# Routing an encoder layer's tokens: router scores taken from x, and the first gathers ahead of the rest of the table

## The chip, the cores and the metric

The kernel runs on one NeuronCore of a Trainium2 chip. The time is the device time of one execution in microseconds (us), and lower is better. The five engines of the core appear here as PE (TensorE, matrix products), DVE (VectorE), ACT (ScalarE), POOL (GpSimd) and SP (SyncE, which here only issues transfers). PEld is PE's loading of stationary operands, and a "q" behind an engine's name (SPq, PEldq) is its instruction sequencer. PE's clock is granted at one of two levels, 2.4 GHz (shown as 1.00) or 1.2 GHz (0.50).

## What is computed

An encoder layer on 768 tokens (256 of a prompt, 512 of a sample) of width 1024, all in fp32. The part that the change touches is the second half, a mixture of experts in two levels:

```
x = x + m @ w_out[l]
h = rms_norm(x, norm2_g[l])
g_logits = h @ w_group + b_group          # 4 groups
e_all    = h @ w_expert + b_expert        # 4 x 8 experts
g_sel = argmax(g_logits); top_v, top_j = top_k(e_logits of the group, 2)
gates = p_g * softmax(top_v)
hid = silu(x_b @ w_gate[e]) * (x_b @ w_up[e])   # per block of gathered rows
y   = hid @ w_down[e]
```

`rms_norm(x, g)` is x times 1/sqrt(mean(x²) + eps), one factor per token, times g, one factor per column.

## The kernel before

Tokens lie in NT = 6 tiles of 128 rows. An attention and a convolution stage fill the first 285 us. Then comes the output product: 24 groups of 12 matmuls each (`out`, line 1143), each adding 512 columns of one tile to `x` through a DVE instruction (`px`, line 1721). When a tile is complete, ACT squares and sums it (`sq2`, L1473), POOL makes the norm's factor `r2` of it in two instructions (`root2`, L851 and L852), DVE writes the normed tile `h2` (L1728), PE transposes it in eight products (`turn_h2`, L1156), ACT copies the transposed tile out of PSUM (`turned_h2`, L1480), and PE multiplies it by the router's weights `wr`, 36 columns (`logits`, L649). SP stores each tile of `h2` twice to `h_rows` in HBM (L770), because rows are gathered from there later. The order of all these steps on each engine comes from `plan()`, a list scheduler with estimated costs: a step is placed when its predecessors are finished by those costs. `tnh`, `tch` and `lgt` are its names for turn, copy and logits.

Where PE has to wait it multiplies constants (`stay_busy(n)`, n products of 128x128, L1163). One such stretch of 16 lies between the last output product and the logits of tile 4.

After the logits (semaphore `lg_done`) DVE and PE take turns for some 25 us: adding the bias (L1802), choosing groups and experts, counting them, ordering the experts by load, and placing each token in a block of 64 rows. The blocks' row lists come out of a one-hot product on PE (L1225, two halves), which raises `idx_ps`. DVE then writes a `table` of integers (L1861 to L1871) with the experts' order, their first blocks and ends, and two loop counts; then it turns the row lists into indices (`idx_of` for the first two blocks, L1876; `idx` for all, L1878); then it computes the gates (to L1888), which PE spreads over the blocks in a second one-hot product (L1233). The table's readers load integers from it into registers (`value_load`): POOL its loop counts (L899, L900), PE the blocks of each expert (L1295, L1296), SP an expert's number and end (L743, L744).

POOL then gathers the first two blocks of rows (L910, an indirect transfer). DVE waits for the gates and the first gather and copies the block (L1935), PE turns it (`turn_rows`, L1240), DVE copies that out (L1897), and PE starts the first expert: gate and up products in two halves of k (L1249, L1252), then the down products (L1286, L1287).

Weights, 6 MB for each of 32 experts, are streamed by SP (L736) into three slots. The first three experts' are loaded ahead: part during the output product, the other 9.5 MB behind the last store of `h2`. Every later load waits for PE to have finished with the slot; the first of them waits for `gu_half`, which PE raises when the first half of the first expert's gate and up products is done.

Of the kernel before, what the change touches and what calls it, by code (L numbers as in the profile page):

```python
# [34 lines left out]
P = 128  # L35
D = 1024
# [123 lines left out]
def parts():  # L160
# [222 lines left out]
def encoder(nc, x_prompt, x_sample, norm1, w_in, rpb, vectors, w_out, norm2, router_w, router_b,  # L383
# [15 lines left out]
    with ExitStack() as ctx:  # L399
# [57 lines left out]
        h2T = mid[:, NT * D:NT * D + 2 * D].rearrange("p (b k n) -> p b k n", b=2, k=KD)  # L457
# [32 lines left out]
        br = sb("br", [P, NR])  # L490
        ident = sb("ident", [P, P])
# [25 lines left out]
        def after(n):  # L517
# [79 lines left out]
        sq2, root2, h2_ready, h2t_done, h2t_ready, lg_done = (  # L597
            sem("sq2"), sem("root2"), sem("h2_ready"), sem("h2t_done"), sem("h2t_ready"), sem("lg_done"))
# [46 lines left out]
        def logits(pe, t):  # L645

            pe.wait_ge(h2t_ready, t + 1)
            for k in range(KD):
                mm = pe.matmul(ps[:, 6, t * NR:(t + 1) * NR], h2T[:, t % 2, k, :], wr[:, k, :],  # L649
                               start=(k == 0), stop=(k == KD - 1))  # L650
            mm.then_inc(lg_done, 1)
# [3 lines left out]
        def _(sp):  # L655
# [18 lines left out]
            sp.dma_start(wr[:], router_w.rearrange("p (k n) -> p k n", k=KD)).then_inc(small_in, 16)  # L674
            sp.dma_start(br[:], bass.AP(router_b.tensor, 0, [[0, P], [1, NR]])).then_inc(small_in, 16)
# [104 lines left out]
            sp.wait_ge(h2t_done, NT)  # L780
# [22 lines left out]
        def _(pool):  # L803
# [181 lines left out]
        def _(pe):  # L985
# [162 lines left out]
            def turn_h2(t):  # L1148
                pe.wait_ge(h2_ready, t + 1)
                if t == 1:  # L1150
                    pe.wait_ge(ssc_ready, 1)
                if t >= 2:
                    pe.wait_ge(h2t_ready, t - 1)
# [4 lines left out]
                mm.then_inc(h2t_done, 1)  # L1158
# [6 lines left out]
            for what, *a in ORDER:  # L1165
# [22 lines left out]
                elif what == "po":  # L1188
                    out(*a)
                    if a[0] == len(OUT) - 1:  # L1190
                        pe.wait_ge(x2_done, max(g for g in range(len(OUT)) if OUT_BANK[g] == 7) + 1)
                        stay_busy(16)
                elif what == "tnh":
                    turn_h2(*a)
# [24 lines left out]
            stay_busy(12)  # L1219
# [8 lines left out]
            stay_busy(8)  # L1228
# [7 lines left out]
            stay_busy(4)  # L1236
# [56 lines left out]
            turn_rows()  # L1293
            def expert(place, s, target):
# [33 lines left out]
        def _(act):  # L1328
# [146 lines left out]
            def turned_h2(t):  # L1475
                act.wait_ge(h2t_done, t + 1)
                if t >= 2:
                    act.wait_ge(lg_done, t - 1)
                bank = 4 * (1 - t % 2)
                nc.scalar.activation(h2T[:, t % 2, :, :].rearrange("p k n -> p (k n)"),  # L1480
                                     ps[:, bank:bank + 2, :].rearrange("p a b -> p (a b)"),
                                     ACT.Copy).then_inc(h2t_ready, 1)

            for what, *a in ORDER:
# [26 lines left out]
                elif what == "sq2":  # L1511
                    squares_of_x2(*a)
                elif what == "tch":
                    turned_h2(*a)
# [54 lines left out]
        def _(dve):  # L1569
# [207 lines left out]
            dve.wait_ge(small_in, 32)  # L1777
# [24 lines left out]
            link(V.tensor_tensor(lg[:], ps[:, 6, 0:NT * NR].rearrange("p (t n) -> p t n", t=NT), same(br[:], NR), ALU.add))  # L1802
# [62 lines left out]

            link(V.tensor_scalar(even[:], even[:], ends[0:1, E:], None, ALU.is_lt))
# [5 lines left out]

            dve.wait_ge(idx_ps, 1)
            link(V.tensor_scalar(nobody[:], ps[0:BLK, 5, 0:NB], 0.0, float(4 * T), ALU.is_equal, ALU.mult))
            for q in range(2):
                V.scalar_tensor_tensor(idx_of[q][:], nobody[:, q:q + 1], -1.0, ps[0:BLK, 5, q:q + 1], ALU.add, ALU.add  # L1876
                                       ).then_inc(idx_ready, 1)
            V.scalar_tensor_tensor(idx[:], nobody[:], -1.0, ps[0:BLK, 5, 0:NB], ALU.add, ALU.add).then_inc(idx_ready, 1)  # L1878
# [144 lines left out]
```

## Time and profile before

| | us |
|---|---|
| median of 3 runs | 938.34 (937.21 to 940.13) |
| profiled execution | 941.61 |
| its span, first to last instruction | 939.8 |
| PE busy in the span | 856.7 |
| DVE busy | 427.1 |
| ACT busy | 249.2 |
| POOL busy | 146.5 |

The profile is of one execution, and times in its views are counted from the start of the span. The other 1.8 us of that execution lie around the span. A share of busy time is a mean over stages with different limits, so it has to be read stage by stage.

### The profile page before, as it was taken

The page shows a single profiled execution, that of the slowest core. Times are in us where ns is not written, and L with a number is a line of the kernel's source. Part 1 is how long each engine was busy: PE and PEld are TensorE (multiplying, and loading weights), DVE is VectorE, ACT ScalarE, POOL GpSimd, SP SyncE. Part 2 cuts the span into 40 slices and gives each one's busy share as a digit, 9 for nine tenths or more (in the row PEclk, how much of TensorE's full clock was granted, in tenths as well). Part 3 has the DMA queues.
Part 4 walks back from the last instruction along what each step waited for, and adds up shares of the span by engine and source line. Part 5 has one row for each costly group of instructions (what it writes and reads, how often), then busy time and mean ns, then how long its engine had stood idle before and what let it go on. Part 6 is the DMA issues. An engine that isn't in the chain of part 4 may idle for free.

```text
span 939.8 us, 16091 instructions
## 1 busy us (share of the span) xinstructions
PE 856.7 (91%) x5980; PEld 588.0 (63%) x5981; DVE 427.1 (45%) x639; ACT 249.2 (27%) x486; POOL 146.5 (16%) x287
## 2 busy tenths in 40 slices
PE   3989999999869999699999789999999999899984
PEld 2879978777648889655554445565555555455541
DVE  5398988866997443622222112222222212222256
ACT  5313164565565122011111011111111111111121
POOL 4200010000000110122221212222122222121203
PEclk9989999999979999989999999999999999999998
DMA  7443445221085355969999999999999999999984
GB/s 204 121 113 102 150 153 190 91 80 45 1 224 224 153 217 193 368 238 404 402 390 395 414 402 399 406 390 397 400 403 410 404 401 379 394 387 407 395 331 137
DMA packets 80892, 265.80 MB, mean 283 GB/s; under 512 B 18089, under 2 KB 43945, under 8 KB 56280
## 3 DMA queue, kind: packets, MB, share of 16 engines
q1 hardware_dynamic: 63232, 245.10, 68.7%
q0 software_dynamic: 7808, 18.56, 5.7%
q10 hardware_dynamic: 9816, 1.66, 1.0%
q8 instruction: 23, 0.38, 0.2%
q14 instruction: 13, 0.11, 0.0%
HBM read 247.52 MB, written 27.08 MB: 292 GB/s over the span
## 4 chain that ended last, share of the span: by engine, by line
PE 51%; DMA 21%; SPq 16%; DVE 7%; issue 3%; ACT 1%; ACTq 0%; POOLq 0%; POOL 0%; DVEq 0%
SPq L736 15%; DMA big<-in_w_up 13%; PE ps L1021 13%; PE ps L1249 7%; PE ps L1143 7%; DMA ring<-in_w_up 6%; PE ps L1286 5%; PE ps L1017 4%; PE ps L1252 3%; DVE big L1637 2%; PE ps L1240 1%; PE ps L1040 1%; PE ps L1070 1%; PE ps L1049 1%; PE ps L649 1%
## 5 line engine op out<-in xcount | busy, mean ns | idle before, releaser
L1252 PE MATMUL ps<-ring,big 128*64 128x256 f32 x704 | 158.4, 383 | 7.1 <-DMA ring<-in_w_up 7.1
L1249 PE MATMUL ps<-ring,big 128*64 128x256 f32 x704 | 158.8, 383 | 1.8 <-DVE big L1897 1.2
L1021 PE MATMUL ps<-hT,w_split 128*128 128x512 f32 (+1 forms) x768 | 145.2, 344 | 4.1 <-DVE hT L1593 3.6
L1908 DVE TENSOR_TENSOR big<-ps,big 64x256 f32<-64x256 f32 x78 | 33.2, 426 | 242.4 <-ACT big L1534 242.4
L1252 PE MATMUL ps<-big 128*64 128x256 f32 x544 | 122.0, 380 | 16.5 <-DMA big<-in_w_up 16.5
L1021 PEld LDWEIGHTS ps<-hT,w_split 128*128 128x128 f32 x768 | 118.0, 190 | 25.6 <-issue 11.3
L1249 PEld LDWEIGHTS ps<-ring,big 128*64 128x64 f32 x704 | 96.8, 138 | 57.7 <-issue 14.1
L1249 PE MATMUL ps<-big 128*64 128x256 f32 x544 | 123.1, 380 | 0.5 <-DMA big<-in_w_gate 0.5
L1637 DVE SCALAR_TENSOR_TENSOR big<-big,vec 128x783 f32<-128x783 f32 x116 | 119.6, 1031 | 3.0
L1252 PEld LDWEIGHTS ps<-ring,big 128*64 128x64 f32 x704 | 96.9, 138 | 14.4 <-DMA ring<-in_w_up 9.4
L1534 ACT ACTIVATE big<-ps 64x256 f32<-64x256 f32 x78 | 29.3, 376 | 268.7 <-PE ps L1252 268.7
L1252 PEld LDWEIGHTS ps<-big 128*64 128x64 f32 x544 | 73.4, 137 | 36.8 <-DMA big<-in_w_up 22.6
L1249 PEld LDWEIGHTS ps<-big 128*64 128x64 f32 x544 | 73.2, 137 | 31.4 <-issue 8.1
L1917 DVE TENSOR_SCALAR big<-ps,gate_of 64x512 f32<-64x512 f32 x39 | 29.5, 756 | 124.4 <-PE ps L1287 124.3
L1286 PE MATMUL ps<-ring,big 128*64 128x512 f32 x176 | 80.4, 599 | 0.1
L1287 PE MATMUL ps<-ring,big 128*64 128x512 f32 x176 | 80.5, 599 | 0.0
L1143 PE MATMUL ps<-wo_split,hT 128*128 128x512 f32 x288 | 70.2, 402 | 2.1 <-issue 2.1
L922 POOL COPY to_of<-idx 64x1 uint32 x37 | 18.8, 508 | 309.8 <-DVE big L1917 309.8
L1143 PEld LDWEIGHTS ps<-wo_split,hT 128*128 128x128 f32 x288 | 54.9, 194 | 13.5 <-issue 2.1
L1286 PE MATMUL ps<-big 128*64 128x512 f32 x136 | 62.3, 599 | 0.1
L1287 PE MATMUL ps<-big 128*64 128x512 f32 x136 | 62.4, 599 | 0.0
L1546 ACT ACTIVATE big<-ps,gate_of 64x512 f32<-64x512 f32 x39 | 26.6, 682 | 131.8 <-PE ps L1287 131.8
(236 smaller groups left out, 1132.5 us busy)
## 6 DMA issues: line engine op xcount, KB each, us to landing
ring<-in_w_gate SPq DMA_DIRECT2D x44, 1024.0 KB, 29.0
ring<-in_w_up SPq DMA_DIRECT2D x44, 1024.0 KB, 29.8
ring<-in_w_down SPq DMA_DIRECT2D x44, 1024.0 KB, 30.1
big<-in_w_gate SPq DMA_DIRECT2D x20, 1024.0 KB, 29.8
big<-in_w_up SPq DMA_DIRECT2D x20, 1024.0 KB, 30.7
big<-in_w_down SPq DMA_DIRECT2D x20, 1024.0 KB, 29.8
w_raw<-in_w_in SPq DMA_DIRECT2D x20, 512.0 KB, 3.9
results<-spare POOLq DMA_DIRECT2D x12, 512.0 KB, 2.9
```

The lines of the kernel that those rows point to most:

```text
L736: sp.dma_start(to[:, ks, :], src).then_inc(landed, 16)
L1017: mm = pe.matmul(ps[:, n % 2, 0:2 * P], hT[:, k // 4, hi_h, k % 4, g * P:(g + 1) * P], split_of(2 * c)[:, :, hi_w, k, :], **flags)
L1021: mm = pe.matmul(ps[:, n % 2, 0:size], w_split[:, sub, hi_w, k, :], hT[:, k // 4, hi_h, k % 4, cols], **flags)
L1143: mm = pe.matmul(ps[:, OUT_BANK[g], :], mT[:, part, hi_m, k, t * P:(t + 1) * P], wo_split[n % 2][:, hi_w, k, :], start=(k == 0 and m == 0) ...
L1249: pe.matmul(ps[0:BLK, 6 * h, 0:FH], xT[:, k, :], gate_w[s][:, k, fs], start=(k == 0), stop=(k == KD - 1))
L1252: mm = pe.matmul(ps[BLK:2 * BLK, 6 * h + 1, 0:FH], xT[:, k, :], up_w[s][:, k, fs], start=(k == 0), stop=(k == KD - 1))
L1286: pe.matmul(ps[0:BLK, 2, :], hbT[:, k, :], down_w[s][:, k, 0:512], start=(k == 0), stop=(k == KF - 1))
L1287: mm = pe.matmul(ps[BLK:2 * BLK, 3, :], hbT[:, k, :], down_w[s][:, k, 512:1024], start=(k == 0), stop=(k == KF - 1))
L1534: nc.scalar.activation(sG[:, h * FH:(h + 1) * FH], ps[0:BLK, 6 * h, 0:FH], ACT.Silu).then_inc(sg_ready[h], 1)
L1637: link(nc.vector.scalar_tensor_tensor(conv[:, j % 2, :], z, w, conv[:, j % 2, :], ALU.mult, ALU.add))
L1908: nc.vector.tensor_tensor(hb[:, fs], ps[BLK:2 * BLK, 6 * h + 1, 0:FH], sG[:, fs], ALU.mult).then_inc(hb_ready[h], 1)
L1917: nc.vector.tensor_scalar(yb2[q][:, 512:1024], ps[BLK:2 * BLK, 3, :], gate_of[q][BLK:2 * BLK], None, ALU.mult).then_inc(evacuated, 1)
```

## The change

The router's scores no longer wait for the norm. PE transposes `x` itself, the norm's column factors are multiplied into `wr` once, and the row factor `r2` is put onto the scores in one more DVE instruction. On DVE the indices come before the last six instructions of the table, and POOL asks for the first two gathers before it loads its loop counts. The counts of `stay_busy` change at five places and one is added. `norm2` is loaded a second time, one factor per partition and chunk (128x8 single values).

```diff
-            in_line(("tnh", t), [("h2", t)] + ([("tch", t - 2)] if t >= 2 else []) + ([("sscc",)] if t == 1 else []))
+            in_line(("tnh", t), [("px", s)] + ([("tch", t - 2)] if t >= 2 else []) + ([("sscc",)] if t == 1 else []))
...
-            pe.wait_ge(h2t_ready, t + 1)
+            pe.wait_ge(x2t_ready, t + 1)
+            if t == 0:
+
+                pe.wait_ge(h2_ready, 1)
...
             sp.dma_start(wr[:], router_w.rearrange("p (k n) -> p k n", k=KD)).then_inc(small_in, 16)
+            sp.dma_start(n2_column[:], bass.AP(norm2.tensor, 0, [[1, P], [P, KD]]), allow_slow_non_contiguous=True).then_inc(small_in, 16)
...
-            pool.wait_ge(table_ready, 1)
-            pairs = pool.value_load(table[0:1, 3 * E:3 * E + 1], min_val=(E - 7) // 2, max_val=MAXPAIRS)
-            rest = pool.value_load(table[0:1, 3 * E + 1:3 * E + 2], min_val=2, max_val=3)
...
             for q in range(2):
                 pool.wait_ge(idx_ready, q + 1)
                 fetch(q)
+            pool.wait_ge(table_ready, 1)
+            pairs = pool.value_load(table[0:1, 3 * E:3 * E + 1], min_val=(E - 7) // 2, max_val=MAXPAIRS)
+            rest = pool.value_load(table[0:1, 3 * E + 1:3 * E + 2], min_val=2, max_val=3)
...
-            def turn_h2(t):
-                pe.wait_ge(h2_ready, t + 1)
+            def turn_x2(t):
+                pe.wait_ge(x2_done, OUT.index((OUT_CHUNKS - 1, t)) + 1)
...
-                                      h2[:, t, k * P:(k + 1) * P], ident[:])
+                                      x[:, t, k * P:(k + 1) * P], ident[:])
...
-                        stay_busy(16)
+                        stay_busy(2)
...
-            stay_busy(12)
+            stay_busy(13)
...
-            stay_busy(8)
+            stay_busy(14)
...
-            stay_busy(4)
+            stay_busy(8)
...
             turn_rows()
+            stay_busy(3)
             def expert(place, s, target):
...
                 if t == 0:
                     dve.wait_ge(norms_in, 16)
+                    dve.wait_ge(small_in, 48)
+                    link(nc.vector.tensor_tensor(wr[:], wr[:], n2_column[:].unsqueeze(2).to_broadcast([P, KD, NR]), ALU.mult))
...
-            link(V.tensor_tensor(lg[:], ps[:, 6, 0:NT * NR].rearrange("p (t n) -> p t n", t=NT), same(br[:], NR), ALU.add))
+
+            link(V.tensor_tensor(lg[:], ps[:, 6, 0:NT * NR].rearrange("p (t n) -> p t n", t=NT), over(r2[:], NR), ALU.mult))
+            link(V.tensor_tensor(lg[:], lg[:], same(br[:], NR), ALU.add))
...
+            dve.wait_ge(idx_ps, 1)
+            link(V.tensor_scalar(nobody[:], ps[0:BLK, 5, 0:NB], 0.0, float(4 * T), ALU.is_equal, ALU.mult))
+            for q in range(2):
+                V.scalar_tensor_tensor(idx_of[q][:], nobody[:, q:q + 1], -1.0, ps[0:BLK, 5, q:q + 1], ALU.add, ALU.add
+                                       ).then_inc(idx_ready, 1)
+            V.scalar_tensor_tensor(idx[:], nobody[:], -1.0, ps[0:BLK, 5, 0:NB], ALU.add, ALU.add).then_inc(idx_ready, 1)
+
             link(V.tensor_scalar(even[:], even[:], ends[0:1, E:], None, ALU.is_lt))
```

PE, from the second half of the output product to the end of the logits (128x512 are output products, 12 to a group; 128x128 from `ident` and `big` or `x` the turns; 128x36 the logits). Before:

```order
L1143 MATMUL ps<-wo_split,hT 128x512 x120
L1156 MATMUL ps<-ident,big 128x128 x8
L1143 MATMUL ps<-wo_split,hT 128x512 x12
L649 MATMUL ps<-wr,big 128x36 x8
L1156 MATMUL ps<-ident,big 128x128 x8
L1143 MATMUL ps<-wo_split,hT 128x512 x12
L649 MATMUL ps<-wr,big 128x36 x8
```

The same place on PE now:

```order
L1147 MATMUL ps<-wo_split,hT 128x512 x108
L1160 MATMUL ps<-ident,x 128x128 x16
L653 MATMUL ps<-wr,big 128x36 x8
L1147 MATMUL ps<-wo_split,hT 128x512 x12
L653 MATMUL ps<-wr,big 128x36 x8
L1147 MATMUL ps<-wo_split,hT 128x512 x24
L1160 MATMUL ps<-ident,x 128x128 x8
```

The turns of tiles 0 and 1 stand together, one group earlier, and the logits of tile 0 directly behind them; before, an output group lay between a turn and its logits. On ACT the copy of tile 0 still stands behind the squares of tile 1:

```order
L1472 ACTIVATE wo_split<-wo_raw 128x2048 x2
L1478 ACTIVATE big,ss<-x 128x1024 x2
L1485 ACTIVATE big<-ps 128x1024 x2
L1478 ACTIVATE big,ss<-x 128x1024
L1485 ACTIVATE big<-ps 128x1024
```

What moved on ACT is only the copy of tile 1, which now follows that of tile 0 at once.

DVE behind the first three instructions of the table, now (before, the rows from `even` to `table<-ends` stood first and those from `nobody` to `idx` last):

```order
L1872 TENSOR_SCALAR table<-ps 1x32
L1875 TENSOR_SCALAR nobody<-ps 64x58
L1877 SCALAR_TENSOR_TENSOR idx_of<-nobody,ps 64x1 x2
L1879 SCALAR_TENSOR_TENSOR idx<-nobody,ps 64x58
L1881 TENSOR_SCALAR even<-even,ends 1x24
L1882 TENSOR_REDUCE cnt<-even 1x1
L1883 SCALAR_TENSOR_TENSOR cnt<-cnt,ends 1x1
L1884 TENSOR_SCALAR cnt<-cnt 1x1
L1885 CAST table<-cnt 1x2
L1886 CAST table<-ends 1x32
```

The indices passed six small instructions, and the table is complete that much later. POOL behind the last root, now:

```order
L911 DMA big<-h_rows,idx_of 64x1024 x2
L936 TENSOR_LOAD table
L936 ISA x2
L937 TENSOR_LOAD table
L937 ISA x2
L917 COPY gate_of<-row_gates 128x1 x2
```

Before, the two loads with their checks stood ahead of the two gathers.

## Rows read from the trace of the kernel before

**Rows 1.** The page, second part: mean busy share of the DMA engines in 40 slices.

```profile
DMA  7443445221085355969999999999999999999984
```

**Rows 2.** Busy time by stretch: PE, PEld, DVE, ACT, POOL, granted clock, DMA share, GB/s.

```profile
800.00:900.00 100.00, 96.17 (x730) 55.98 (x728) 24.81 (x43) 15.54 (x39) 16.99 (x33) 1.00 1.00 397
```

**Rows 3.** SP's queue in order of time: start, us, transfers issued.

```profile
374.31 1.09 SPq L736 DMA_DIRECT2D big<-in_w_down  x2
408.73 0.36 SPq L736 DMA_DIRECT2D ring<-in_w_gate  x1
...
420.73 0.34 SPq L736 DMA_DIRECT2D ring<-in_w_gate  x1
```

**Rows 4.** The chain that ended last, around the logits: start, us, work.

```profile
332.41 0.88 PE ps L1156 x8
...
363.00 3.57 PE ps L1163 x32
...
369.22 1.03 ACT big L1480
370.30 1.99 PE ps L649 x16
372.31 0.40 DVE lg L1802
```

**Rows 5.** DVE and ACT in order of time, around tile 1's completion.

```profile
329.72 0.75 DVE L1721 SCALAR_TENSOR_TENSOR x<-ps,rc,x 128x512 f32<-128x512 f32 x1 [1.97 <-PE ps L1143]
...
331.48 0.18 ACT L1473 ACTIVATION_READ_ACCUMULATOR big<-x 128x1 f32 x1
```

**Rows 6.** PE and DVE in order of time, around the index.

```profile
390.55 0.91 PE L1225 MATMUL ps<-big,spare 128*64 128x58 f32 x24 [0.54 <-DVE big L1858]
...
390.82 0.18 DVE L1864 TENSOR_SCALAR table<-ps 1x32 int32<-1x32 f32 x1
...
392.14 0.20 DVE L1874 TENSOR_SCALAR nobody<-ps 64x58 f32<-64x58 f32 x1
392.38 0.21 DVE L1876 SCALAR_TENSOR_TENSOR idx_of<-nobody,ps 64x1 uint32<-64x1 f32 x2
```

**Rows 7.** The chain again, from the first gather to the first expert.

```profile
394.56 4.93 DMA big<-h_rows,idx_of
...
399.58 0.70 DVE spare L1935
...
402.76 0.68 PE ps L1249
```

**Rows 8.** Who waited for whom (us in total, times), and the gathers' landing times.

```profile
POOL big L910 <- POOL idx_of L903: 31.4, 37, 0.9
...
DMA to landing us min/median/max: 3.5/7.2/8.2
```

**Rows 9.** PE in order of time and its granted clock by 1 us (columns of Rows 2).

```profile
396.37 1.16 PE L1163 MATMUL ps<-lane,ident 128*128 128x128 f32 x8
400.41 1.11 PE L1240 MATMUL ps<-ident,spare 64*128 64x64 f32 x8 [2.88 <-DVE spare L1935]
...
416.91 0.38 PE L1249 MATMUL ps<-ring,big 128*64 128x256 f32 x1
...
400.00:401.00 1.00, 0.59 (x6) 0.62 (x6) 0.27 (x1) 0.00 (x0) 0.18 (x1) 0.62 0.00 0
...
407.00:408.00 1.00, 1.00 (x12) 0.63 (x10) 0.00 (x0) 0.00 (x0) 0.00 (x0) 0.96 0.00 0
```

**Rows 10.** PE's sequencer at the table: durations in ns (min/median/max), first and last start.

```profile
L1295 PEldq TENSOR_LOAD <-table x32: 298/303/502, 400.7 to 890.8; - x32
```

**Rows 11.** SP's queue at the start, and its loads of 1024 runs of 512 bytes.

```profile
33.76 0.48 SPq L676 DMA_DIRECT2D n<-in_norm  x1
39.59 28.35 SPq L661 DMA_DIRECT2D w_raw<-in_w_in  x5
...
L661 SPq DMA_DIRECT2D w_raw<-in_w_in x20: 367/373/596, 4.0 to 197.0; - x20
```

More of the change, by code:

```diff
@@ L456, in encoder @@
         h2 = mid[:, 0:NT * D].rearrange("p (t d) -> p t d", t=NT)
-        h2T = mid[:, NT * D:NT * D + 2 * D].rearrange("p (b k n) -> p b k n", b=2, k=KD)
+        x2T = mid[:, NT * D:NT * D + 2 * D].rearrange("p (b k n) -> p b k n", b=2, k=KD)
         slot2_gu, slot2_dn = big[:, (NT + 2) * D:(NT + 2) * D + 2 * KD * F], big[:, 0:KF * D]
@@ L490, in encoder @@
         br = sb("br", [P, NR])
+        n2_column = sb("n2_column", [P, KD])
         ident = sb("ident", [P, P])
@@ L596, in encoder @@
         wout_done, x2_done = sem("wout_done"), sem("x2_done")
-        sq2, root2, h2_ready, h2t_done, h2t_ready, lg_done = (
-            sem("sq2"), sem("root2"), sem("h2_ready"), sem("h2t_done"), sem("h2t_ready"), sem("lg_done"))
+        sq2, root2, h2_ready, x2t_done, x2t_ready, lg_done = (
+            sem("sq2"), sem("root2"), sem("h2_ready"), sem("x2t_done"), sem("x2t_ready"), sem("lg_done"))
         gd_ready, ge_ready, order_ready, order_ps, dd_ready, ex_ready, dest_ready, table_ready = (
@@ L645, in logits @@
         def logits(pe, t):
-            pe.wait_ge(h2t_ready, t + 1)
+            pe.wait_ge(x2t_ready, t + 1)
+            if t == 0:
+                pe.wait_ge(h2_ready, 1)
             for k in range(KD):
-                mm = pe.matmul(ps[:, 6, t * NR:(t + 1) * NR], h2T[:, t % 2, k, :], wr[:, k, :],
+                mm = pe.matmul(ps[:, 6, t * NR:(t + 1) * NR], x2T[:, t % 2, k, :], wr[:, k, :],
                                start=(k == 0), stop=(k == KD - 1))
@@ L779, in _ @@
             sp.wait_ge(h2_out, 32 * NT)
-            sp.wait_ge(h2t_done, NT)
+            sp.wait_ge(x2t_done, NT)
             load_some(2, 2, 4, 6)
@@ L1152, in turn_h2 @@
                 if t >= 2:
-                    pe.wait_ge(h2t_ready, t - 1)
+                    pe.wait_ge(x2t_ready, t - 1)
                 bank = 4 * (1 - t % 2)
@@ L1156, in turn_h2 @@
                     mm = pe.transpose(ps[:, bank + k // 4, (k % 4) * P:(k % 4 + 1) * P],
-                                      h2[:, t, k * P:(k + 1) * P], ident[:])
-                mm.then_inc(h2t_done, 1)
+                                      x[:, t, k * P:(k + 1) * P], ident[:])
+                mm.then_inc(x2t_done, 1)
             def stay_busy(products):
@@ L1191, in _ @@
                         pe.wait_ge(x2_done, max(g for g in range(len(OUT)) if OUT_BANK[g] == 7) + 1)
-                        stay_busy(16)
+                        stay_busy(2)
                 elif what == "tnh":
-                    turn_h2(*a)
+                    turn_x2(*a)
                     if a[0] == NT - 1:
@@ L1473, in squares_of_x2, with turned_x2 @@
                 nc.scalar.activation(junk, x[:, t, :], ACT.Square, accum_out=ss2[:, t:t + 1]).then_inc(sq2, 1)
-            def turned_h2(t):
-                act.wait_ge(h2t_done, t + 1)
+            def turned_x2(t):
+                act.wait_ge(x2t_done, t + 1)
                 if t >= 2:
@@ L1479, in turned_h2 @@
                 bank = 4 * (1 - t % 2)
-                nc.scalar.activation(h2T[:, t % 2, :, :].rearrange("p k n -> p (k n)"),
+                nc.scalar.activation(x2T[:, t % 2, :, :].rearrange("p k n -> p (k n)"),
                                      ps[:, bank:bank + 2, :].rearrange("p a b -> p (a b)"),
-                                     ACT.Copy).then_inc(h2t_ready, 1)
+                                     ACT.Copy).then_inc(x2t_ready, 1)
             for what, *a in ORDER:
@@ L1513, in _ @@
                 elif what == "tch":
-                    turned_h2(*a)
+                    turned_x2(*a)
             act.wait_ge(gd_ready, 1)
@@ L1776, in _ @@
             dve.wait_ge(lg_done, NT)
-            dve.wait_ge(small_in, 32)
             V = nc.vector
@@ L1871, in _ @@
             V.tensor_copy(table[0:1, 2 * E:3 * E], ends[0:1, 1:]).then_inc(table_ready, 1)
[L1873 to L1878, printed above, removed]
             dve.wait_ge(ge_ready, 1)
```

## The prediction, made before the result was known

> **What bounds the kernel now.** I read the page first, by slices [rows 1]: the DMA engines are only half busy before the experts (digits 3, 5, 5, 3 around 290 to 380 us), and from slice 18 to the end full. The table by stretch says the same [rows 2]: from 800 to 900 us their share is 1.00 at some 400 GB/s. PE is nearly full too (96 of 100 us), but it has what the weights give it. So from the first reload of weights on, the bytes that are left set the end, and what a change ahead of it is worth is read at one instant: SP's first reload, at 408.73 us [rows 3]. Whatever moves this instant moves the end by as much.
>
> Then I went back from it. The reload waits for half of the first expert's gate and up products, which start at 402.76 [rows 7]. They wait for the first gather, which is asked for at 394.56 and lands 4.93 us later. That one waits for the index, and this for the 18 us of turns between DVE and PE behind the logits, whose first instruction is at 372.31 [rows 4]. The change touches the logits, the index and the gather. I take them in this order.
>
> **Ahead of the last output group: a new stall.** The output product runs on PE without a gap. Group 15, tile 1's last, ends as its DVE instruction starts, 329.72 [rows 5]. Behind it PE now has the turns of tiles 0 and 1, 0.88 each [rows 4], done at 331.47, and then at once the logits of tile 0. These need ACT's copy of tile 0, and ACT has the squares of tile 1 first, which end at 331.48 + 0.18 = 331.66 [rows 5]. The copy takes 1.03, and PE followed such a copy 0.05 later [rows 4]: 332.74. PE stands for 1.27 us, and as nothing else was idle there, the last output group ends that much later. Before, an output group stood in between. The wait of tile 0's logits for `wr` and `h2` is covered: one multiplication of 128x288, between the 0.40 of the 128x216 one [rows 4] and perhaps 0.6, and one norm are done before 332.7. The later turns have a group between themselves and their copies: no stall. Cost: **+1.27**.
>
> **Behind it: 14 products less.** Between the last output group and the first table instruction PE is the late one: 16 products of constants take 3.57 us [rows 4], 0.223 each, then the logits of tile 4, the turn of tile 5, its copy, its logits. With 2 products instead of 16, 3.12 us go. What could be late next: the turn of tile 5 needs the last `px`, 0.8 us after the group; PE comes to it after 0.45 + 1.7. The copy of tile 5 needs ACT, busy with the squares until 2.0 after the group, while the turn ends at 3.0. The norm of tile 5, no longer in the way of PE, is done by DVE before the logits are. So the whole is won: **-3.12**. The scores get one more DVE instruction of the same size: 0.40 plus the 0.02 between two: **+0.42**. The chain behind it starts 1.43 us earlier, and its steps up to the index are unchanged: the fillers of 28, 6 and 13 products still end before what they wait for.
>
> **The index.** The second half of the index product runs from 390.55 to 391.46; DVE has finished the three table instructions at 391.00 and now takes the index at 391.50 instead of 392.14 [rows 6]. `idx_of` follows 0.24 later and is written at 391.9. POOL, now without table loads ahead, asks 0.85 us after its index is ready (31.4 us in 37 waits, [rows 8]): 392.75 instead of 394.56, **-1.81**. With the 1.43 the first gather is asked for at 391.32.
>
> **The landing.** Here the gain shrinks. The 4.93 us were measured at the end of the weights loaded ahead; the last of these are issued at 374.31 and after [rows 3]. They stand behind the norm of tile 5, so they move by the stall, 1.27 us later, while the gather moves 3.2 us forward, into their midst. Landings range from 3.5 to 8.2 us, with a median of 7.2, which stands for a full DMA [rows 8]. I take 7.2, since at 391 the engines are as full as in the expert phase: 398.52 instead of 399.49, **-0.97**. No row shows this first gather inside the burst, and 4.93 is the other value it can have; that is the first rival.
>
> The Trainium skill, page "DMA: Bandwidth & Descriptors", section "Queues, rings and completion order", says that a DMA engine goes round its queues packet by packet. By that rule a gather of few packets should pass the weights with little delay, which would give the first rival's time. The median of 7.2 in a full phase speaks against it.
>
> **From landing to the first product.** The block's copy starts at 399.58 and PE at 402.76 [rows 7], 3.18 later. Its sequencer loads the expert's numbers from 400.7 on [rows 10], while the turns of rows run (400.41, [rows 9]) and behind them, and I take these loads, two of 0.3 us with their checks, to be what is late rather than DVE's copy. The 3 new products stand ahead of them: at least their issue (12 instructions at the pace of the 16 that were issued in 0.3 us, 0.2), at most their run, 0.67. I take **+0.2**, as the sequencer is seen running ahead of the array. The Trainium skill, page "TensorE: Matmul & The Clock Gate", section "Architectural detail: the array is 16x 32x32, not 1x 128x128", gives PE's queue a depth of 64, which would hold all of them; with a queue that does not, it would be 0.67.
>
> **The clock.** The granted clock falls at 400.4, after 2.9 us without products, and is back at 407 [rows 9]. The first half of gate and up, 402.76 to SP's issue at 408.73, therefore takes 5.97; the next block, at full clock, takes 420.73 - 416.91 = 3.82 [rows 3, 9]. If the clock stays up, **-2.15**. The fillers grew for this: 14 products (3.1 us) behind the index, 8 (1.8 us) behind the gates. By my times the gate product ends at 395.4 (396.37 less 1.43, plus 0.46 for the instructions that now stand ahead of the gates), the filler at 397.2, and the turn of rows comes at 399.4: 2.2 us empty, and then 0.9 us more before the first expert. That is less than the 2.9 that preceded the fall, in the longest piece. I expect it to hold, with little room.
>
> **The rest.** The column load is 1024 runs of 4 bytes; loads of 1024 runs of 512 bytes are issued in 0.37 to 0.60 us, and SP has 5.3 us free there (34.24 to 39.59, [rows 11]). Between nothing and 5 us it is hidden, and it is first used 290 us later. Gates come 0.46 us later than the index gain alone would give, hidden by the landing. The table is ready later too; SP uses it only for the reload.
>
> **The sum.** Landing -0.97, three products +0.2, clock -2.15: the reload is issued at 405.8 instead of 408.7, **-2.9**. Against the profiled execution (941.61) that is 938.7. This execution was 3.3 above the median of the runs, so against the median, 938.34, it is **935.4**.
>
> **Rivals.**
> 1. *The gather passes the weights.* At 4.93 it lands at 396.3, and then PE's filler of 8 is late instead: the turn of rows cannot start before 397.2, 3.2 earlier than before. With +0.2 and the clock certainly held, -5.2: **933.1**. For it: this gather has no scatter in its own queue. Against: 7.2 in the full phase.
> 2. *The clock falls after all*, since 2.2 and 0.9 us are still empty. The gather's -0.97 and the +0.2 remain, -0.8, if the low stretch again lies half over the waits; if it falls only as the first expert starts, all 16 steps run low, 6.9 instead of 6.0, and it is +0.1 to +0.5. **938.2**, between 937.5 and 938.8.
> 3. *Slower: the weights ahead hold the gather back to the end.* The gather asked in mid-burst lands only when the burst, 1.27 us later than before, is through: 8.2 us (the longest row), 399.5. The same 2.9 us are then empty, the clock falls, later than before against the first expert, which runs 6.9 low, and the three products cost 0.67: 0 + 0.7 + 0.9 = +1.6, **939.9**. It decides against the change from a landing of 8 us on.
> 4. *The earlier reload does not reach the end.* If PE, at 96%, set the pace of the expert phase through its own work, it would still shift with its start; only a stall inside would eat the gain. **938.3**.
>
> **Chances.** Forecast 0.38, rival 1 0.24, rival 2 0.27, rival 3 0.07, rival 4 0.04. A measurement of this kernel can tell about 0.3%, 2.8 us, from no change. Rival 1 lies beyond it, the forecast just beyond (a little over half of it counts as faster), rivals 2 and 4 within, rival 3 within but for a spread of 1 to 2 us on top. Faster 0.47, same 0.46, slower 0.07. The range goes from rival 1 less 0.8 to rival 2's upper end plus 0.4: 932.3 to 939.2.
>
> **What the profile after would show.** PE idle for about 1.3 us at tile 0's logits, near 331.5, waiting for ACT. The first score instruction near 370.5, the index near 390.1, the first gather near 391.3 with a landing of 7 (rival 1: 5; rival 3: over 8). Granted clock 1.00 up to the first expert (rival 2: 0.50 there). SP's first reload near 405.8, and a DMA share of 1.0 from then on. The prediction is wrong if the stall is not there (1.3 better), if the routing chain between scores and index changed, or if the reload moves and the end does not.

## The result, and the profile after

The changed kernel takes **942.25 us** (median of 17 runs, 940.73 to 943.97) beside 938.99 for the kernel before (17 runs, 937.21 to 941.19). The ratio is 1.0033 (95% interval 1.0024 to 1.0042): slower by 3.3 us. 935.4 had been forecast, with a range up to 939.2. The profiled execution took 942.78 us with a span of 940.9, near the median. That of before, on which the sum was made, was 2.6 us above its median. One execution of a kernel shown further down (burst split, no stall) took 1233.76 us at a mean granted clock of 0.656; it is among the nine of that kernel's median (935.14), but not in its ratio.

First the instant that was to tell everything, SP's queue of the changed kernel in order of time (start, us, transfers issued); it answers to [rows 3]:

```profile
361.62 8.96 SPq L775 DMA_DIRECT2D h_rows<-big  x4
370.63 2.61 SPq L741 DMA_DIRECT2D ring<-in_w_up  x1
...
377.26 0.88 SPq L741 DMA_DIRECT2D big<-in_w_down  x2
410.46 0.36 SPq L741 DMA_DIRECT2D ring<-in_w_gate  x1
```

The first reload is issued at 410.46, where 405.8 was expected and before had 408.73. From there to the end of the span it is 530.4 us; before it was 531.1, and in all 14 traces of this document it lies between 529.5 and 531.1. So the step that whatever moves the reload moves the end by as much holds, and the loss lies ahead of it.

Next the chain that ended last (start, us, work), which answers to [rows 4, 7]:

```profile
330.62 0.76 DVE x L1726
...
331.40 1.15 ACT big L1478 x2
332.55 0.92 ACT big L1485
...
333.51 1.98 PE ps L653 x16
335.49 2.85 PE ps L1147 x12
...
365.56 0.44 PE ps L1167 x4
...
371.75 0.39 DVE lg L1809
...
384.87 4.64 PE ps L1167 x26
389.52 0.84 PE ps L1229 x24
...
391.42 0.22 DVE nobody L1875
...
392.78 8.39 DMA big<-h_rows,idx_of
...
401.26 0.70 DVE spare L1943
...
402.09 1.11 PE ps L1244 x8
403.20 1.58 PE ps L1167 x6
404.78 0.62 PE ps L1253
```

Three places differ from the forecast. The stall at tile 0's logits is there, as forecast (333.51). The gather is asked for 1.78 us earlier than before, but takes 8.39 us to land and arrives at 401.17, where before it arrived at 399.49. And the three new products (`L1167 x6`, each product has two records) take 1.58 us and end just before the first expert starts.

The windows of the changed kernel show what the gather waited for (columns of [rows 2]: PE, PEld, DVE, ACT, POOL, granted clock, DMA share, GB/s):

```profile
392.00:393.00 1.00, 1.00 (x11) 1.00 (x10) 0.83 (x6) 0.00 (x0) 0.22 (x1) 1.00 1.03 414
398.00:399.00 1.00, 1.00 (x10) 0.86 (x8) 0.00 (x0) 0.00 (x0) 0.00 (x0) 1.00 0.98 270
399.00:400.00 1.00, 0.05 (x1) 0.00 (x0) 0.00 (x0) 0.00 (x0) 0.00 (x0) 1.00 0.72 176
400.00:401.00 1.00, 0.00 (x0) 0.00 (x0) 0.00 (x0) 0.00 (x0) 0.00 (x0) 1.00 0.09 21
402.00:403.00 1.00, 0.91 (x8) 0.94 (x8) 0.00 (x0) 0.00 (x0) 0.18 (x1) 0.50 0.00 0
```

The DMA engines are full until 399, nearly empty from 400, and the gather's data is there 1 us after. The trace also has the packets by queue. q1 carries what SP issues, q0 the gathers (packets, MB, share of the 16 engines; first from 396 to 397, then from 397 to 398):

```profile
q1 hardware_dynamic: 56, 0.43, 100.8%
...
q1 hardware_dynamic: 40, 0.32, 86.9%
q0 software_dynamic: 20, 0.07, 19.6%
```

Until 397 the engines move no packet of the gather that was asked for at 392.78; from 397 on its packets go beside the last weights. Its first packet comes 4.3 us after the request, where in the kernel before it came 1.9 us after. So it did not pass the weights ahead of it; it came in at their end. PE has nothing to do meanwhile, and its clock is at the lower level when the rows are turned.

### The profile page after: what moved, and what is told of

The parts are those of the page before. It is cut to its first block, busy times and chain, and to the rows that moved or that the text cites. A ratio compares the mean times of both kernels' runs of the same rounds, so it can differ in the third digit from the quotient of the medians.

```text
span 940.9 us, 16096 instructions
## 1 busy us (share of the span) xinstructions
PE 860.8 (91%) x5980; PEld 591.6 (63%) x5981; DVE 428.4 (46%) x641; ACT 248.8 (26%) x486; POOL 146.1 (16%) x287
## 3 DMA queue, kind: packets, MB, share of 16 engines
q10 hardware_dynamic: 9816, 1.66, 0.9%
## 4 chain that ended last, share of the span: by engine, by line
PE 53%; DMA 24%; SPq 12%; DVE 6%; issue 2%; ACT 1%; ACTq 0%; POOL 0%; POOLq 0%; DVEq 0%
DMA big<-in_w_up 16%; PE ps L1025 13%; SPq L741 11%; PE ps L1253 8%; PE ps L1147 7%; PE ps L1290 5%; PE ps L1021 4%; DMA big<-in_w_down 3%; DMA ring<-in_w_up 3%; PE ps L1256 3%; DVE big L1642 2%; PE ps L1244 1%; PE ps L1044 1%; PE ps L1074 1%; PE ps L1053 1%
```

## The experiments

Where a time is given in the table, it comes from one profiled execution of each kernel. "Last output" is the start of the last `px` instruction of DVE, "asked" POOL's first gather, "landed" when its data was there (0.09 us before DVE's copy of the block starts, but for the last row, where the copy waited for something else), "reload" SP's first reload, "ratio" the time against the kernel before on the same chip.

| kernel | last output | asked | landed | first expert | reload | ratio (95%) |
|---|---|---|---|---|---|---|
| before | 363.04 | 394.56 | 399.49 | 402.76 | 408.73 | 1 |
| before, again | 362.89 | 394.43 | 397.70 | 400.80 | 406.20 | 0.9998 (0.9983-1.0013) |
| second part alone | 363.49 | 393.37 | 399.03 | 402.29 | 408.74 | 1.0007 (0.9990-1.0024) |
| after | 365.60 | 392.78 | 401.17 | 404.71 | 410.46 | 1.0033 (1.0024-1.0042) |
| after, first part alone | 363.32 | 392.23 | 399.13 | 402.43 | 407.98 | 1.0030 (1.0017-1.0043) |
| after, old fillers | 365.13 | 392.30 | 400.59 | 403.71 | 409.65 | 1.0024 (1.0013-1.0035) |
| after, no stall | 362.61 | 389.77 | 398.24 | 401.79 | 407.80 | 1.0007 (0.9993-1.0021) |
| before, burst held | 364.02 | 395.56 | 402.32 | 405.59 | 410.96 | 1.0041 (1.0026-1.0057) |
| before, burst early | 362.15 | 393.69 | 396.70 | 399.97 | 405.31 | 0.9996 (0.9987-1.0005) |
| after, burst early | 365.36 | 392.51 | 399.27 | 402.57 | 407.56 | 1.0005 (0.9994-1.0016) |
| the same, no stall | 364.06 | 391.25 | 398.50 | 401.79 | 407.07 | 0.9988 (0.9977-0.9999) |
| after, burst split, no stall | 363.07 | 390.25 | 395.12 | 398.42 | 402.28 | 0.9960 (0.9946-0.9975) |
| the same, smaller fillers | 364.67 | 391.86 | 396.76 | 399.87 | 403.73 | 0.9960 (0.9944-0.9976) |
| before, split, second part | 363.40 | 393.31 | 396.4 | 400.82 | 406.37 | 0.9987 (0.9975-0.9999) |

Single executions of one kernel differ by more than the effects looked for: the two of the kernel before lie 2.5 us apart at the reload, and the start of tile 1's last `px` lies between 328.4 and 330.7 us in the 14 traces without regard to the change. So I use differences inside one trace, and the ratios for the sum.

**The kernel before, once more.** No edit.

> The kernel before, unchanged, for a second trace. If its first profiled execution (2.6 us above its own median) was an unlucky one, this trace shows SP's first reload earlier than 408.7 us, by up to 2.6 us, and names the place: the clock kept at 1.00 through the first expert (2.2 us less) or an earlier start of the output product's second half. If the first trace was typical, the reload is again at 408 to 409. The time is the kernel before's, ratio 1.000.

938.16 us in the profiled execution, 939.31 in the median of 12. POOL's queue in its trace:

```profile
394.43 1.20 POOL L910 DMA_INDIRECT big<-h_rows,idx_of  x1 [28.69 <-issue]
```

The chain of the same trace:

```profile
394.43 3.27 DMA big<-h_rows,idx_of
...
397.79 0.70 DVE spare L1935
```

The same gather of the same code, asked for at the same time, landed in 3.27 instead of 4.93 us. So 4.93 is not fixed by the request.

**The stall undone.** The logits of tile 0 go back behind an output group; nothing else changes.

```diff
 ORDER = plan()
+ORDER.remove(("lgt", 0))
+ORDER.insert(ORDER.index(("po", 16)) + 1, ("lgt", 0))
```

> The changed kernel with the logits of tile 0 one output group later on PE; nothing else differs. Theory of the stall (PE waits 1.3 us for ACT's copy): the idle time at these logits goes to 0, the last output group ends 1.3 us earlier and the time falls from +3.3 us over the kernel before to +2.0. Rival (the gather's landing inside the weights' burst takes all that comes ahead of it): the burst starts 1.3 us earlier too, so the gather lands 1.3 us earlier as well, and again +2.0; only if the landing is held by the burst's end and the burst does not move with the stall does it stay at +3.3.

The ratio falls from 1.0033 to 1.0007, where 2.0 us over the kernel before (1.002) had been expected, so the stall carries the larger part of the loss. Its trace, the chain:

```profile
389.77 8.47 DMA big<-h_rows,idx_of
...
398.33 0.70 DVE spare L1945
```

The gather was asked for 4.7 us earlier than in the kernel before (again), and landed 0.5 us later. A request moved by this much without effect says that something else sets the landing.

**The two parts taken apart.** First the changed kernel with its second part undone (indices behind the whole table, POOL's loads ahead of the gathers):

```diff
+            pool.wait_ge(table_ready, 1)
+            pairs = pool.value_load(table[0:1, 3 * E:3 * E + 1], min_val=(E - 7) // 2, max_val=MAXPAIRS)
+            rest = pool.value_load(table[0:1, 3 * E + 1:3 * E + 2], min_val=2, max_val=3)
             pool.wait_ge(zero_out, 16 * ZERO_TILES)
...
-            dve.wait_ge(idx_ps, 1)
-            link(V.tensor_scalar(nobody[:], ps[0:BLK, 5, 0:NB], 0.0, float(4 * T), ALU.is_equal, ALU.mult))
```

> The changed kernel with the second part undone: the table whole ahead of the indices, POOL's loop counts loaded ahead of the first two gathers. Theory (the earlier gathers only wait longer in the burst of weights): asked for 1.8 us later, the gather lands at the same time within 0.5 us, its landing 6.6 instead of 8.4 us, and the time is that of the changed kernel, +3.3 us over the kernel before, or up to 0.5 less since the gates come 0.5 earlier. Rival (the earlier request is worth its 1.8 us): +5 us over the kernel before.

1.0030, as slow as the whole change. Then the kernel before with the second part alone (the same lines the other way round):

> The kernel before with the second part of the change alone: indices ahead of the table's rest, both gathers ahead of POOL's loop counts; router, order and fillers as before. Theory (held by the burst): asked for at 392.8 instead of 394.6, it lands at 399 to 399.5 with 6.5 us, a gain of 0 to 0.5 us; ratio 0.9995 to 1.000. Rival (worth its 1.8 us): lands at 397.7, ratio 0.998. If the added order does harm (both gathers into the burst): above 1.001.

1.0007, no difference from the kernel before that these runs can tell. Its gather is asked for 63.20 us after tile 1's last `px` (before, again: 64.86), so the part does what it is meant to; it lands 35.5 us after the last output instruction, as the others do. The loss is the first part's, and the second part brings nothing that can be told: the earlier request did not bring an earlier landing.

**The burst moved ahead.** The seven loads of weights (7 MB) that stand behind the last store of `h2` go ahead of tile 5's two stores. In the changed kernel, in the changed kernel without the stall, and in the kernel before:

```diff
             for t in range(NT):
+                if t == NT - 1:
+                    sp.wait_ge(wout_done, NT * OUT_CHUNKS)
+                    for e in range(2):
+                        for l in pieces[e]:
+                            if l not in early[e]:
+                                load(e, *l)
                 sp.wait_ge(h2_ready, t + 1)
```

> The changed kernel with the seven weight loads (7 MB) issued ahead of the last tile's stores instead of behind them; they then wait for the last output group, not for tile 5's norm. In the six traces so far the first gather landed 28.9 to 30.8 us after the first of these loads was issued, whether it was asked for at 389.8 or at 394.6 us. Theory (the weights' burst decides the landing): the burst starts 4 to 5 us earlier and has drained at about 393, the gather lands 3.3 to 5 us after it is asked for, near 396.5 instead of 401.2, and the time falls by 3 to 5 us, to 0.998 to 1.000 of the kernel before. Rival (a gather beside other transfers takes 7 to 8 us by itself): landing at 400 to 401, ratio 1.003 as the changed kernel. The stall and the fillers stay as they are.

> The same with the logits of tile 0 one output group later too. Theory: both gains add, 1.3 to 2.4 us more than the loads moved alone, 0.995 to 0.998 of the kernel before; the first gather then lands before PE's filler of 8 products ends, and this filler or the gates' product sets the turn of rows. Rival (the landing no longer matters once it is early): no further gain, equal to the loads moved alone.

> The kernel before with the seven weight loads ahead of the last tile's stores, nothing else. Its gather is asked for at 394.5, when a burst that started 4 us earlier has drained. Theory (the burst held this landing as well): lands at 3.3 to 3.6 us in every execution (4.9 and 3.3 in the two traces), time 0.998 to 0.999 of the kernel before. Rival (the request itself, behind the table, set it): no change, 1.000.

Starting the burst earlier (365.35 instead of 370.63) takes the changed kernel from 1.0033 to 1.0005, without an earlier request. That is less than was expected of it (a landing near 396.5; it was 399.27), and without the stall the expected 0.995 to 0.998 became 0.9988. The kernel before gains nothing that can be told (0.9996), though the weights were through just behind the request (DMA share 0.00 from 394 to 395). Its DVE in order of time, and then its windows (columns as above):

```profile
396.79 0.68 DVE L1936 COPY spare<-big 64x1024 f32<-64x1024 f32 x1 [2.88 <-DMA big<-h_rows,idx_of]
```

```profile
393.00:394.00 1.00, 0.04 (x2) 0.04 (x2) 0.88 (x1) 0.00 (x0) 0.31 (x1) 1.00 0.82 344
394.00:395.00 1.00, 1.00 (x36) 1.00 (x37) 0.00 (x0) 0.00 (x0) 0.89 (x1) 1.00 0.00 0
```

Asked for at 393.69, it took 3.0 us with the burst through: the least of all 14 traces. In the changed kernel the gather still stood beside weights, and SP's queue with the early burst shows which:

```profile
369.55 0.81 SPq L781 DMA_DIRECT2D h_rows<-big  x2
...
390.68 1.03 SPq L741 DMA_DIRECT2D big<-in_w_down  x2
```

The last two loads (`big<-in_w_down`, 2 MB) wait until the stores have landed. The stores now stood behind 7 MB of weights, the second landed 21 us after its issue, and let these loads go at 390.68, just ahead of the gather, after the engines had run nearly empty (share 0.07 to 0.13 from 389 to 392). The gather landed in 6.76 us.

**The old fillers.** The changed kernel with 12, 8 and 4 products again, and without the three behind the rows' turn:

```diff
-            stay_busy(13)
+            stay_busy(12)
...
-            stay_busy(14)
+            stay_busy(8)
...
-            stay_busy(8)
+            stay_busy(4)
...
             turn_rows()
-            stay_busy(3)
```

> The changed kernel with four of its fillers as before: 12, 8, 4 and none instead of 13, 14, 8 and 3 products (the 2 instead of 16 stays). Theory of the landing: fillers hide in the wait for the gather; the three products ahead of the first expert cost 0.3 us at half clock and the 13 hold the index product back 0.6 us at half clock, while the gather lands with the burst anyway: 0 to -0.6 us against the changed kernel, 1.002 to 1.0035 of the kernel before. Rival (the fillers are what costs): back to 1.000. If they kept the clock up in some executions: slower than the changed kernel by up to 2 us.

1.0024 against 1.0033, with intervals that overlap. The added products carry at most some 2 us of the loss, by the ratios, and their help does not show, nor a harm that these runs can tell. From the landing to the first expert it is 3.12 us here and 3.54 in the changed kernel.

**The burst held back.** The opposite test, on the kernel before: the seven loads also wait for the last logits.

```diff
             sp.wait_ge(wout_done, NT * OUT_CHUNKS)
+            sp.wait_ge(lg_done, NT)
```

> The kernel before with one wait more: SP issues the weights loaded ahead only when all logits are done (372.3 us) instead of behind the last stores (369.3 us); routing, gather request and fillers unchanged. Theory (the gather lands when this burst has drained): burst, landing and first reload all 2.5 to 3 us later, time 1.0025 to 1.0035 of the kernel before, with the gather asked for at the same 394.5 us. Rival (burst does not matter): landing within 0.5 us of before, 1.000.

The routing chain is untouched: from the last output instruction to the request it is 31.54 us, as in the other two traces of this kernel (31.52 and 31.54). The burst starts 9.3 us after that instruction instead of 6.3 and 6.0, the gather lands 38.3 us after it instead of 36.5 and 34.8, and the kernel is 3.7 us slower (1.0041, interval 1.0026 to 1.0057; 1.0025 to 1.0035 was expected). So later weights alone make this kernel slower, by about as much as they are late.

**The burst split.** Three of the seven loads ahead of tile 5's stores and four behind them, so that the stores land early and neither the engines nor the last two loads wait. With the stall undone:

```diff
+            left = [(e, l) for e in range(2) for l in pieces[e] if l not in early[e]]
             for t in range(NT):
+                if t == NT - 1:
+                    sp.wait_ge(wout_done, NT * OUT_CHUNKS)
+                    for e, l in left[:3]:
+                        load(e, *l)
                 sp.wait_ge(h2_ready, t + 1)
...
+            for e, l in left[3:]:
+                load(e, *l)
```

> The changed kernel with the logits of tile 0 one output group later and three of the seven weight loads (3 MB) ahead of the last tile's stores, four behind. With all seven ahead DMA stood idle for 3 us near 389 and the slot-2 loads, issued at 390, met the gather. Theory: the burst now runs without that gap and has drained by 390, the gather, asked for at 391.2, lands within 3.0 to 3.6 us at 394.6, and the turn of rows comes when PE's filler of 8 products ends, at 397.5; reload near 404.5 to 405.5, 0.996 to 0.998 of the kernel before. Rival (a fixed 7 us for a gather asked for this early): landing 398.5, 0.999.

**935.14 us, ratio 0.9960 (0.9946 to 0.9975)**: faster than both kernels. The gather took 4.87 us, not the 3.0 to 3.6 expected. SP's queue in its trace:

```profile
363.07 0.33 SPq L743 DMA_DIRECT2D ring<-in_w_up  x1
...
377.61 0.80 SPq L743 DMA_DIRECT2D big<-in_w_down  x2
402.28 0.36 SPq L743 DMA_DIRECT2D ring<-in_w_gate  x1
```

Its PE in order of time, at the end of the wait for the gather:

```profile
394.46 2.05 PE L1171 MATMUL ps<-lane,ident 128*128 128x128 f32 x16
396.45 1.10 PE L1248 MATMUL ps<-ident,spare 64*128 64x64 f32 x8
397.47 0.94 PE L1171 MATMUL ps<-lane,ident 128*128 128x128 f32 x6
398.42 0.42 PE L1257 MATMUL ps<-ring,big 128*64 128x256 f32 x1
```

PE has no gap any more: the gather is there (DVE's copy starts at 395.21) before the filler of 8 ends, the clock stays at the upper level, and the first expert reaches the reload in 3.86 us instead of 5.75. This is what the forecast had described, with the engines drained three microseconds earlier (DMA share 0.18 from 394 to 395). The chain that ended last no longer has the gather in it: it goes through the gates on DVE, their product on PE (392.92) and the filler behind it.

The same with fillers of 4 and none behind the gates and the rows' turn:

> The same with 4 instead of 8 products behind the gates' product and none ahead of the first expert. Theory: 0.9 us less of filler in front of the turn of rows, which is now set by the gates' product and the block's copy, and 0.2 to 0.3 less ahead of the first expert: 0.5 to 1.2 us faster than with the long fillers, if the clock does not fall earlier for it; if it does, up to 2 us slower. Rival (filler hidden as before): no difference.

0.9960 again, and again 3.86 us from first expert to reload, where a gain of 0.5 to 1.2 us was expected. So with the gather early the last two fillers need not be larger for the clock. The 14 products behind the index stand in both kernels, and no run takes them away here. And the split with the second part on the kernel before, without the router's part:

> The kernel before with the change's second part (indices first, gathers ahead of the loop counts) and three of the seven loads ahead of the last stores. The request at 393.2 us now meets a drained burst. Theory: landing in 3.0 to 3.6 us at 396.5, against 396.8 to 399.5 so far, time 0.9975 to 0.999 of the kernel before, where the second part alone gave 1.0007. Rival: the second part is worth nothing even so, 0.9996 as with the loads moved alone.

0.9987 (0.9975 to 0.9999). The request here comes at 393.31, when the engines are nearly empty (share 0.26 from 392 to 393, 0.10 to 394), and the gather lands 3.1 us later, near 396.4, as expected. DVE's copy of the block waits longer all the same, and not for the gather:

```profile
397.64 0.69 DVE L1937 COPY spare<-big 64x1024 f32<-64x1024 f32 x1 [1.72 <-PE ps L1235]
```

It waits for the gates' product, which the second part has moved back by 0.8 us (it starts 23.3 us after the first score instruction, with the early burst alone 22.5). Counted from the same instruction, the landing is 1.6 us earlier than with the early burst alone (23.7 against 25.3), the copy only 0.4 (25.0 against 25.4). With the burst out of the way the gates are the next limit.

PE's clock is at 0.53 from 401 to 402, and from first expert to reload it is 5.55 us. The router's part, rid of its stall and with its fillers, is thus worth some 2.5 us by the ratios (0.9960 against 0.9987, with intervals that touch). Of this the clock is 1.7 us (5.55 against 3.86), and whether it stays up for the earlier scores or for the 14 instead of 8 products behind the index no run separates.

## Why the prediction was wrong, step by step

**Where the sum missed.** The forecast put the reload 76.1 us after tile 1's last `px` (79.0 before, less 2.9); it came 79.84 after. Of the 3.75 us between them 0.56 lies ahead of the request, 1.19 in the landing (8.39 instead of 7.2), 0.07 between landing and first expert, and 1.93 in the clock (-0.22 instead of -2.15). The two steps that failed are the landing and the clock behind it.

**The stall: right in kind and size, wrong in reach.** PE in order of time, which answers to [rows 5]:

```profile
330.42 2.10 PE L1160 MATMUL ps<-ident,x 128*128 128x128 f32 x16
333.51 1.75 PE L653 MATMUL ps<-wr,big 128*128 128x36 f32 x14 [1.00 <-ACT big L1485]
```

Forecast was 1.27, measured is 1.00 in front of the logits, which start 2.89 us after tile 1's last `px` (forecast 3.02). But from that `px` to the last output instruction it is 34.98 us instead of 33.32: 1.66. Two things come on top. Logits behind a wait take 1.98 us and not the 1.71 of those behind other products (in the chain, 333.51 and 366.01), 0.27 more. And an output group directly behind logits takes 2.85 where one behind a turn takes 2.74; there are four such groups now instead of one, 0.33 more. With the 1.00 this makes 1.60 of the 1.66. The sum priced neither.

**14 products less: right.** From the last `px` to the first score instruction it is 6.15 us instead of 9.27, that is 3.12 less, as forecast. With the extra DVE instruction (0.39 + 0.02, forecast 0.42) and the 1.66, the chain starts 1.05 us earlier instead of 1.43.

**The index: right.** The request comes 62.16 us after tile 1's last `px` instead of 64.84, 2.68 earlier; forecast was 3.24. Of the difference 0.38 is the chain's later start, and 0.18 is left for the index term (1.63 instead of 1.81). One thing on this way was not foreseen: the filler of 13 products ahead of the index product takes 4.64 us (384.87 to 389.51), because the granted clock was at the lower level from 384 to 388. A low stretch there is in seven of the eight traces with the router's part, where 14 products less stand ahead of the turns between DVE and PE, and in none of the six without it. It cost nothing: from the first score instruction to the index (391.42) it is 19.67 us here and 19.70 in the eighth trace, whose clock stayed up.

**The landing: the first step that failed.** It was counted from the request: 7.2 us, taken from the gathers of the full phase [rows 8]. Here the end of the burst decides. In seven traces with the burst behind the stores, the landing follows the last output instruction by 34.8 to 36.5 us (401.17 - 365.60 = 35.57 in the changed kernel, 399.49 - 363.04 = 36.45 before), whether the request comes 27.2 us after that instruction or 31.5. The other way round, seven traces have the request at the same place, 27.15 to 27.19 us after it, and three arrangements of the weights. The gather takes 8.3 to 8.5 us with the burst behind the stores, 6.8 and 7.2 with all of it ahead, and 4.9 with it split. I had written that the last weights "move by the stall, 1.27 us later", and then did not add the 1.27 to the time at which the weights are through. With the landing tied to the burst, the first part gives +1.66 and the second nothing, where the sum had -0.97 for both. Rival 3 had this mechanism, with a chance of 0.07 and a price of +1.6, of which the landing was 0: it too counted 8.2 us from the request. The runs showed +3.3.

The Trainium skill, page "DMA: Bandwidth & Descriptors", section "Queues, rings and completion order", has the engines go round their queues packet by packet. This gather is no simple case of it: until 397 the engines moved none of its packets, and only then did both queues run side by side. What holds the first packet back for 4.3 us no run here separates. Nor does a gather always wait for the end of the weights. In the expert phase the gathers land after 7.2 us in the median, while a weight load issued by SP there takes some 29 us:

```profile
ring<-in_w_gate SPq DMA_DIRECT2D x44, 1024.0 KB, 29.0
```

So there the gathers land long before loads that were issued ahead of them. The 7.2 speaks against a landing in 4.9, as the forecast has it, but not against passing the weights. A request far ahead of the burst's end might land before that end too; here the earliest came 8.5 us before its landing, and no run moved it further.

**From landing to first product: the cover was too thin.** The sequencer's loads were to hide the three products (+0.2). The sequencer's first load is at 402.49, ahead of the products, as expected, but the chain shows the products last, 403.20 to 404.78, at the lower clock. From landing to first expert it is 3.54 us instead of 3.27: +0.27, inside the bounds given. Without them it was 3.12.

**The clock: the second step that failed.** It was to stay up (-2.15). It fell, after the gather had left PE idle for 3.04 us ahead of the rows' turn (402.09), longer than the 2.88 of [rows 9] and not 2.2. First expert to reload took 5.75 us (before 5.97). The forecast's -2.15 came about only in the two split kernels with the router's part: 3.86 us. Comparing this one idle stretch with 2.88 is not enough, though. In the kernel before with the early burst PE idles only 0.96 us ahead of the turn, and the clock falls all the same (0.80 from 399 to 400, 5.34 us to the reload). Which idle time decides is open.

**The base.** The reload at 408.73 was that of an execution 2.6 us above its median. I corrected the end for it, but not the parts: in the second trace of the same kernel the gather landed in 3.27 us and the low clock lasted from 400 to 404, not to 407. That execution took 938.16 us, nearer to the median. So part of what the change was to win, the kernel before already had in it.

**The sum.** Inside the traces, the reload lies 79.8, 79.6 and 79.5 us after tile 1's last `px` in the three kernels with the stall and the burst behind it, and 79.0, 76.6 and 78.6 in the three without the router's part (before twice, second part alone): 1.6 more on average, about the 1.66 of the last output instruction. The changed kernel without the stall has 78.9. The ratios of the same kernels give 2.7 against 0.2 us. About 1 us of the loss is thus not accounted for by these averages. The single traces differ among themselves by more than that: against the second trace of the kernel before alone, the changed kernel's reload is 3.2 us later. It remains open. The mean granted clock of whole executions was lower too, 0.978 in the 17 runs of the changed kernel beside 0.981 to 0.982 of the kernel before, of which the new low stretch around 385 is one part.

## What to carry to other kernels

Before an earlier request is credited with an earlier arrival, look at what the DMA engines are doing when it is made. If they are full, and the backlog ends within the time that a gather takes beside one (here up to 8.5 us), expect the arrival at its end, and move the backlog's start or size instead of the request. If the backlog goes on longer, as in the expert phase here, expect it by the request (6.5 to 8.2 us behind it from 420 us on in the kernel before). A stall put ahead of a backlog's start can then cost its full length at the far end, even where the routing chain itself got shorter. And once the transfer is early, look for what is late next; here it was the gates. Last, take the same instant from a second execution before subtracting from it: here two traces of the unchanged kernel lay 2.5 us apart at the reload, and the whole effect was 3.3.

## What the runs showed of the hardware

- A gather of 64 rows landed in 3.0 and 3.1 us when the burst was through or nearly so, in 3.3 and 4.9 when asked for as it ended, and in 5.7 to 8.5 when asked for further ahead of its end. In six traces with the burst behind the stores (changed kernel, no stall, old fillers, first part alone, second part alone, burst held) it landed 0.6 to 2.3 us after the start of the first microsecond with a DMA share below 0.2.
- Its first packet came 1.8 to 1.9 us after the request in the six traces where the burst was ending or over (landings 3.0 to 4.9), and 4.3 to 4.4 us after it in the five where the landing took 6.8 to 8.5 from a request 27.2 us behind the last output instruction.
- Filler products follow the clock: 13 of them took 4.64 us where their full-clock price (0.223 each, [rows 4]) is 2.9, and three took 1.58 instead of 0.67. The three stand in the chain that ended last: a filler that is to keep the clock up can become the late work itself.
- With the stores of `h2` queued behind 7 MB of weights on the same queue, they landed 18 and 21 us after their issue, and while the loads behind them waited, the DMA engines were nearly empty for three microseconds (share 0.07 to 0.13) in the middle of the burst.
